# Hybrid attention with whole 128-partition query operands, scaled probabilities and an output that is made already turned

## The reference, cut to what matters

```python
o_a = chunk_relpos_attention(...)      # 6 heads, a bias by relative position
o_b = dsa_attention(...)               # 5 heads, keys chosen by an index score (top 64)
o_c = mla_attention(...)               # 5 heads of 64 + 32 (rope), latent keys and values
x = x + jnp.concatenate([o_a, o_b, o_c], axis=-1) @ w_out
# each of them, per head:
s = q @ k.T * scale (+ bias or mask);  p = softmax(s);  o = p @ v
```

## Time and profile before

| | |
|---|---|
| three runs | 2169.07, 2173.31, 2173.80 us, median 2173.31 |
| span of the profiled execution | 2100.8 us |
| what lies around the span, against the median | 72.5 us |
| TensorE busy | 1862.9 us (89%), VectorE 1389.1 (66%), ScalarE 745.2 (35%), GpSimd 551.5 (26%) |
| mean granted TensorE clock | 0.981 of 2.4 GHz |
| attention stage of layer 1, from score(0) to the last piece | 289.6 to 383.1 us |
| the same of layer 2 | 850.8 to 942.8 us |

### The profile page before, as it was taken

The page is one execution under the profiler, slowest core; times in us unless marked ns, Lnnn a source line. Parts: engine busy times, 40 slices in busy tenths (PEclk is TensorE's granted clock), DMA queues, the critical chain, the costliest instruction groups (busy, mean ns, idle before and its releaser), DMA issues. The chain is left out here.

```text
span 2100.8 us, 26928 instructions
## 1 busy us (share of the span) xinstructions
PE 1862.9 (89%) x10536; PEld 1428.1 (68%) x10536; DVE 1389.1 (66%) x2647; ACT 745.2 (35%) x1170; POOL 551.5 (26%) x610
## 2 busy tenths in 40 slices
PE   7999999999999999999999999897777777777776
PEld 6999887799989998869898799686322222222222
DVE  5697564667667755647776577779865756757445
ACT  5333545533353444555334444431211111211111
POOL 0000212000000003200000000006777777777772
PEclk9999999999999999999999999998899999999999
DMA  7675441567556754227574132059999999999996
GB/s 263 206 233 184 142 147 61 169 207 240 187 193 227 243 178 148 97 62 244 198 230 146 61 121 88 21 153 401 409 409 409 409 409 410 410 409 409 409 409 272
DMA packets 260499, 505.53 MB, mean 241 GB/s; under 512 B 12340, under 2 KB 178966, under 8 KB 260374
## 3 DMA queue, kind: packets, MB, share of 16 engines
q1 hardware_dynamic: 186438, 235.29, 34.1%
q0 software_dynamic: 73728, 268.47, 32.1%
q10 hardware_dynamic: 208, 0.06, 0.0%
HBM read 502.72 MB, written 1.05 MB: 240 GB/s over the span
## 5 line engine op out<-in xcount | busy, mean ns | idle before, releaser
L277 DVE TENSOR_TENSOR LOWS<-RAW,HIGH 128x2048 fp32r<-128x2048 f32 (+2 forms) x150 | 345.0, 2309 | 36.4 <-ACT HIGH L265 35.8
L265 ACT ACTIVATE HIGH<-RAW 128x2048 fp32r<-128x2048 f32 (+2 forms) x150 | 287.7, 1926 | 135.0 <-DMA RAW<-in_ffn_w_down 41.9
L286 PE MATMUL PB<-HTR,HIGH 128*128 128x256 f32 (+2 forms) x1088 | 313.9, 288 | 0.0
L287 PE MATMUL PB<-HTR,HIGH 128*128 128x256 f32 (+2 forms) x1088 | 311.7, 286 | 0.0
L288 PE MATMUL PB<-HTR,LOWS 128*128 128x256 f32 (+2 forms) x1088 | 311.1, 286 | 0.0
L2470 PE MATMUL PB<-RAW,HTF 128*128 128x512 f32 x432 | 212.1, 617 | 83.4 <-DMA RAW<-in_peer_v,BIG 53.9
L2470 PE MATMUL PB<-HIF,HTF 128*128 128x512 f32 x440 | 215.9, 615 | 72.1 <-DMA HIF<-in_peer_v,BIG 51.8
L2743 POOL DMA_INDIRECT RAW<-in_peer_u,BIG x111 | 105.1, 947 | 558.8 <-DVE BIG L2533 525.2
L2470 PEld LDWEIGHTS PB<-RAW,HTF 128*128 128x128 f32 x432 | 75.5, 192 | 219.7 <-issue 118.5
L2714 ACT ACTIVATE HTF<-CST,BIG 128x128 f32<-128x128 f32 x240 | 91.6, 398 | 369.9 <-PE PB L2470 355.9
L2470 PEld LDWEIGHTS PB<-HIF,HTF 128*128 128x128 f32 x440 | 75.6, 190 | 210.8 <-ACT HTF L2714 114.1
(11 more groups left out here) (402 smaller groups left out, 4083.5 us busy)
## 6 DMA issues: line engine op xcount, KB each, us to landing
RAW<-in_ffn_w_gate SPq DMA_DIRECT2D x32, 1024.0 KB, 6.1
RAW<-in_ffn_w_up SPq DMA_DIRECT2D x32, 1024.0 KB, 6.7
RAW<-in_ffn_w_down SPq DMA_DIRECT2D x32, 1024.0 KB, 5.7
RAW<-in_w_in SPq DMA_DIRECT2D x23, 1120.0 KB, 5.8
RAW<-in_w_mod SPq DMA_DIRECT2D x20, 1024.0 KB, 5.3
BIG<-in_ffn_w_gate SPq DMA_DIRECT2D x12, 1024.0 KB, 6.3
BIG<-in_ffn_w_up SPq DMA_DIRECT2D x12, 1024.0 KB, 8.5
BIG<-in_ffn_w_down SPq DMA_DIRECT2D x12, 1024.0 KB, 5.3
```

Of the source, the lines that this page charges most:

```text
L265: e.activation(u.h, u.raw, ACT.Copy).then_inc(*high_done.up())
L277: e.tensor_tensor(u.l, u.raw, u.h.bitcast(F32), ALU.subtract).then_inc(*low_done.up())
L286: e.matmul(o, lh, rh, start=k == 0, stop=False)
L287: e.matmul(o, lh, rl, start=False, stop=False)
```

## The change

- Queries of kinds A and B are written as whole 128-partition operands: a copy per head of the two, in which the other head's 64 partitions are multiplied by 0 and its own by 0.125 (`HEAD_SCALE`, a column pair set at the start). Keys stay two heads to an operand. Each score product now reads 128 partitions.
- A new step `norm`: VectorE forms 1/sum and multiplies the probabilities by it before they are transposed. probs(i) waits for `att_normed` instead of `att_exp`.
- `sum` swaps its operands: the values of two heads (128 columns) are the stationary operand, the transposed probabilities the moving one (256 and 128 columns), so the output comes out turned. The head's own 64 partitions of it (`UPPER`) are rounded by ScalarE and subtracted by VectorE, per head. The step `turn` is gone, and with it the wait of score(i) for `ot_low`.
- probs(i) waits for `ot_low` of head i-2, since sum writes where the transposes stood.
- Six buffers for the halves of the output instead of four; the tile work at the turns is a step `halves` in slots 4, 7, 11 and 15.
- Pieces per slot by a table, `PIECES_AT` (3, 3, 3, 2, 3, 2, 3, 2, 2 for slots 7 to 15), and two pieces between probs(15) and sum(15).

```diff
+            e.memset(HEAD_SCALE, 0.0).then_inc(*v_step.up())
+            e.wait_ge(*v_step.last())
+            for x in range(2):
+                e.memset(HEAD_SCALE[64 * x:64 * x + 64, x:x + 1], 0.125)
...
+        AQ = Region(BIG, HN_AT, WB_AT)(6, 256)
+        AQ_HALVES = AQ[:, 0:3, :], AQ[:, 3:6, :]
+        BQ_HALVES = FREED[:, 0:3, :], FREED[:, 14:16, :]
+        tail = Region(BIGR, HN_AT + 1536, WB_AT)(2, 256)
+        OT = [(tail[:, 0, :], tail[:, 1, :]), (FREER[:, 0, :], FREER[:, 1, :])] + \
+            [(FREEDR[:, 6 + i, :], FREEDR[:, 10 + i, :]) for i in range(4)]
...
-            PAIRS.append((AQ[r, h // 2, :], AK[r, h // 2, :], [[(J_R, x[:, 128 * (1 - b):256]) for x in (HIGH_OF[h], BIAS_LOW[:, h, :])]
+            PAIRS.append((AQ_HALVES[h % 2][:, h // 2, :], AK[:, h // 2, :],
...
+        PIECES_AT = {7: 3, 8: 3, 9: 3, 10: 2, 11: 3, 12: 2, 13: 3, 14: 2, 15: 2}
+        HALVES_AT = {4: 0, 7: 1, 11: 2, 15: 3}
         pieces_ = []
-        for i in range(NP + 1):
+        for i in range(NP):
             if i + 1 < NP:
                 ORDER.append(("score", i + 1))
-            ready = pieces_[:3 if i < NP else 4] if i > 6 else []
-            pieces_ = pieces_[len(ready):]
-            if i in TURN_AT:
-                ORDER.append(("turn", TURN_AT[i], i))
-                pieces_ += [("piece", TURN_AT[i], b, h) for b in range(2) for h in range(2)]
+            ORDER.append(("norm", i))
+            if i in HALVES_AT:
+                ORDER.append(("halves", HALVES_AT[i]))
+            if i > 2 and i % 2:
+                pieces_ += [("piece", (i - 3) // 2, b, h) for b in range(2) for h in range(2)]
             if i > 0:
                 ORDER.append(("sum", i - 1))
...
-                    if i - 2 in TURN_AT:
-                        e.wait_ge(ot_low.sem, 8 * l + TURN_AT[i - 2] + 1)
...
-                    e.wait_ge(att_exp.sem, base + i + 1)
+                    e.wait_ge(att_normed.sem, base + i + 1)
...
-                        e.wait_ge(att_out.sem, base + i - 1)
+                        e.wait_ge(ot_low.sem, base + i - 1)
...
-                    e.matmul(turned_bank(i)[:, 384:448], P_T[:, i % 2, 0:128], v[0], start=True, stop=True)
-                    e.matmul(turned_bank(i)[:, 448:512], P_T[:, i % 2, 128:256], v[0], start=True, stop=False)
-                    e.matmul(turned_bank(i)[:, 448:512], P_T[:, i % 2, 256:384], v[1], start=False,
+                    e.matmul(turned_bank(i)[:, 0:256], v[0], P_T[:, i % 2, 0:256], start=True, stop=False)
+                    e.matmul(turned_bank(i)[:, 128:256], v[1], P_T[:, i % 2, 256:384], start=False,
                              stop=True).then_inc(*att_summed.up())
...
+                    for b in range(2):
+                        p = P_EXP[:, i % 2, PART[b]]
+                        x = e.tensor_scalar(p, p, RECIP[:, i % 2, b:b + 1], None, ALU.mult)
+                    x.then_inc(*att_normed.up())
...
+                elif what == "sum":
+                    i = a[0]
+                    m, r = i // 2, slice(64 * UPPER[i], 64 * UPPER[i] + 64)
+                    e.wait_ge(att_summed.sem, base + i + 1)
+                    if m >= 6:
+                        e.wait_ge(chunk_done.sem, 8 * l + m - 5)
+                    e.activation(OT[m % 6][0][r, :], turned_bank(i)[r, 0:256], ACT.Copy).then_inc(*ot_high.up())
```

More of the change, by code:

```diff
@@ L850, in build @@
                 4: [("heads", 4, 7), ("heads", 7, 10)], 6: [("heads", 10, 14)]}
-        TURN_AT = {max(4, 2 * m + 3): m for m in range(8)}
+        PIECES_AT = {7: 3, 8: 3, 9: 3, 10: 2, 11: 3, 12: 2, 13: 3, 14: 2, 15: 2}
+        HALVES_AT = {4: 0, 7: 1, 11: 2, 15: 3}
         pieces_ = []
-        for i in range(NP + 1):
+        for i in range(NP):
             if i + 1 < NP:
                 ORDER.append(("score", i + 1))
-            ready = pieces_[:3 if i < NP else 4] if i > 6 else []
-            pieces_ = pieces_[len(ready):]
-            if i in TURN_AT:
-                ORDER.append(("turn", TURN_AT[i], i))
-                pieces_ += [("piece", TURN_AT[i], b, h) for b in range(2) for h in range(2)]
+            ORDER.append(("norm", i))
[3 more added lines that the diff above has]
+                pieces_ += [("piece", (i - 3) // 2, b, h) for b in range(2) for h in range(2)]
             if i > 0:
                 ORDER.append(("sum", i - 1))
[L864 to L867, removed]
+            ORDER += FILL.get(i, []) + pieces_[:PIECES_AT.get(i, 0)]
+            pieces_ = pieces_[PIECES_AT.get(i, 0):]
+            ORDER.append(("probs", i))
+        ORDER += pieces_[:2] + [("sum", NP - 1)] + pieces_[2:] + [("piece", 7, b, h) for b in range(2) for h in range(2)]
         def hybrid_tensor(e, l):
@@ L998, in hybrid_tensor @@
                     v = PAIRS[i][3]
[L999 to L1001 removed]
+                    e.matmul(turned_bank(i)[:, 0:256], v[0], P_T[:, i % 2, 0:256], start=True, stop=False)
+                    e.matmul(turned_bank(i)[:, 128:256], v[1], P_T[:, i % 2, 256:384], start=False,
                              stop=True).then_inc(*att_summed.up())
[L1003 to L1011 removed]
+                elif what == "piece":
                     m, b, h = a
@@ L1176, in hybrid_vector @@
                         selection(a[0])
-                elif what == "sum":
+                elif what == "norm":
                     i = a[0]
@@ L1181, in hybrid_vector @@
                     e.wait_ge(*v_step.last())
[L1182 to L1187 removed]
+                    for b in range(2):
[4 more added lines that the diff above has]
+                    i = a[0]
+                    r = slice(64 * UPPER[i], 64 * UPPER[i] + 64)
+                    oh, ol = OT[i // 2 % 6]
                     e.wait_ge(*ot_high.next())
[L1189 removed]
+                    e.tensor_tensor(ol[r, :], turned_bank(i)[r, 0:256], oh[r, :].bitcast(F32),
                                     ALU.subtract).then_inc(*ot_low.up())
[L1191 to L1192 removed]
+                elif what == "halves":
+                    lows(e, t["out"][a[0]])
             for b in range(2):
@@ L1251, in hybrid_scalar @@
                     e.activation(P_T[:, i % 2, :], turned_bank(i)[:, 0:384], ACT.Copy).then_inc(*att_copied.up())
-                elif what == "turn":
-                    m, i = a
-                    e.wait_ge(*ot_turned.next())
-                    if m >= 4:
-                        e.wait_ge(chunk_done.sem, 8 * l + m - 3)
-                    e.activation(OTH[:, m % 4, :], score_bank(i)[:, 0:256], ACT.Copy).then_inc(*ot_high.up())
-                    if m % 2 == 0:
-                        highs(e, t["out"][m // 2])
+                elif what == "sum":
+                    i = a[0]
+                    m, r = i // 2, slice(64 * UPPER[i], 64 * UPPER[i] + 64)
[3 more added lines that the diff above has]
+                    e.activation(OT[m % 6][0][r, :], turned_bank(i)[r, 0:256], ACT.Copy).then_inc(*ot_high.up())
+                elif what == "halves":
+                    highs(e, t["out"][a[0]])
         def hybrid_gpsimd(e, l):
```

93 lines of the change are left out of this document (41 added, 52 removed).

## The result

The kernel after takes 2147.16 us (median of four runs, 2146.25 to 2148.81), the kernel before on the same chip 2173.56: a ratio of 0.9879 (95%: 0.9865 to 0.9893), 26.4 us less. Forecast were 2157.3 and 16.0 less: the direction was right, the gain too small, the time 0.8 us under the range. On two other chips the same pair gave 20.7 (2178.27 to 2157.60, ratio 0.9910, 0.9894 to 0.9926) and 24.6 us (2102.21 to 2077.62, 0.9878, 0.9862 to 0.9895).

The account below looks back on a forecast made before the run. TensorE's queue was taken to bound the attention stage. Per layer -2.5 + 0.5 + 1.8 - 7.8 = -8.0 us, two layers -16.0: span 2100.8 to 2084.8, with 72.5 around it 2157.3; range 2148 to 2167.

Parts of the forecast that it names:

- Part 3: Each layer's stretch from probs(9) to the last piece: 37.90 us before, forecast 30.1, so -7.8.
- each step from fp32 to fp32r as 0.08 more: On TensorE, each step from an fp32 product to an fp32r one was priced at 0.08 us, two steps per score.
- The 0.32 of the first piece product: Kind B pieces on TensorE: the first takes 0.32 us because it follows a plain fp32 product, the others 0.233.
- the rivals' prices: Two alternatives priced over 22 scores: saving nothing there, +10.2 us, or steps to fp32r costing nothing, 3.5 us.
- part 1: Each layer's stretch from score(0) to probs(4), forecast at -2.5 us, with sum(3) and turn(0) counted as nothing.
- more gain: Steps to fp32r cost nothing (0.16 in 22 scores, 3.5 us) and the clock stays high: 2150, chance 0.10.
- The clock: slot 7's nine products run at the half clock: After waits of 1.8 and 1.6 us within 8 us, slot 7's nine products cost 0.2 more each, +1.8 a layer.
- part 2: Each layer's stretch from probs(4) to probs(9): +0.5 us, as waits take two turns' gain, plus 1.8 of clock.
- The rival of the interleaving: Interleaved fp32r products, not the 64 rows, make scores dear, so 22 scores save nothing: 2167.5, chance 0.13.

Follow-up runs that it names:

- added_x2: The kernel after with every bias and mask product of a score issued twice; its two layers take 86.05 and 84.18 us, against 81.35 and 81.53.
- rows64: The kernel after with scores of kinds A and B reading only their own head's 64 partitions, as before; 2094.20 us, ratio 0.9967 to the kernel before.

## Why the prediction missed

- **Direction, place and mechanism were right.** The gain is TensorE's in the layers, and it comes out at the end. Part 3 holds most of it, norm is covered outside slot 5, sum(6) came 10.8 behind probs(4) (10.1 forecast), probs(5) 4.6 (4.4), waits at sums 11, 14 and 15 were 0.42, 0.58 and 0.20 (0.2, 0.74, 0.3).
- **The step that failed: "each step from fp32 to fp32r as 0.08 more"**, a term mis-sized. The 0.32 of the first piece product was read as a cost. It is where the record puts the start: after, the sum in front is 0.57, not 0.65, and 0.57 and 0.32 are the price of both without a step. added_x2 bears this out: it puts an added product at 0.113 (kind A) and 0.115 (kind B), and 0.65 with four or two of them makes 1.10 and 0.88, where 1.11 and 0.89 were measured, with no room for a step: the term should have been 0. So 0.16 too much stood in each of the 20 scores that the sum counts (3.2 us; the rivals' prices say 22, though the sum gives score(0) nothing) and 0.08 in each slot where pieces follow a sum, together 0.25 for each of five slots in part 3 (3.51 to 3.27, 4.21 to 3.96). In part 1 slot 4's wait, 2.96 instead of 2.50, took part of it. The rival "more gain" (2150, chance 0.10) was the nearest case.
- **"The clock: slot 7's nine products run at the half clock", 1.8 a layer**, did not happen in the profile beside the result, and did in a later one, at 1.6. What was missing is that in the three profiles of the kernel after it is paid there or in slots 4 and 5, so that it moves the layer by 0.3. With what was mis-sized in part 2, that is 1.0 to 1.4 a layer.
- **Not forecast:** in the first layer the kernel before spends 1.5 more ahead of probs(0) than in the second (8.48 against 6.97) at a fallen clock; rows64 has the same difference (10.01 against 8.46), the kernel after in none of its three profiles (6.50 to 6.53). The forecast counted the layers as equal. It also had nothing outside the layers, where 4.0 more came; with the layers' 22.5 alone the time would have been 2151.1, inside the range.
- **The rival of the interleaving** fell: the scores save 0.64 and 0.63, more than the forecast's 0.46. What it has right is that the bias and mask products matter, not by their type but by their 128 rows: with them the 64 rows cost 0.72 a slot, without them about 0.40.

## What to carry to other kernels

Price an operation by the distance between two neighbours of the same kind several operations apart (slot to slot), not by the one recorded start behind it: a 0.08 shift of a start, taken for a cost in 40 places and again in each sum, was the largest error here. A difference of two slots is a price only if neither slot waits: check that each product starts when the one before it is through, and not when another engine's result lands, even where the profile shows no idle time. What is dear about half the rows is each change to them and back, so count the changes before packing or padding. And when a wait of the bounding engine goes back to another engine's queue, move that engine's work that nobody is waiting for (here a weight's rounding) out from ahead of what somebody is.

## What was not expected of the hardware

A change between products of 64 and of 128 rows cost about 0.2 us: two a slot about 0.40, four 0.72. An fp32r product behind a plain fp32 one cost no more than one behind its like, 0.11 to 0.12. An idle time of 2.71 left TensorE's clock high twice, and one of 1.83 was once followed by the half clock. The same kernel before took 2101 us on some chips and 2173 to 2178 on others, all of it in the peer stage (687 against some 760).
